# Half of the value transposes moved behind the diagonal products, two groups of the projection later

## The reference

```
def hgrn_branch(h, w_in, lb, g_onorm, w_out, s0):
    proj = h @ w_in                                  # (T, 4096): q, f, value, z
    q, fpre, inp, z = jnp.split(proj, 4, axis=-1)
    ...                                              # gates, 8 heads of 128 columns
    o, S = hgrn2_chunked(q, k, v, log_f, s0)         # o_t = q_t S_t, S_t = diag(f_t) S_{t-1} + k_t^T v_t
    o = rms_norm(o, g_onorm).reshape(b, T, BRANCH)
    return (o * jax.nn.silu(z)) @ w_out, S
```

## Time and profile before

| | |
|---|---|
| median of three executions | 1053.92 us |
| the profiled execution | 1053.46 us |
| its span on the core | 1051.7 us, so 1.76 us lie around it |
| TensorE busy | 1036.7 us, 99% |
| VectorE busy | 718.3 us, 68% |
| ScalarE busy | 378.4 us, 36% |
| chain that ended last | 91% TensorE, 5% VectorE |

### The profile page before, as it was taken

One profiled execution on the slowest core, in us unless ns is written; L12 is line 12 of the kernel. 1 busy time (PEld: TensorE's weight loads), 2 busy tenths in 40 slices (PEclk: granted clock), 3 DMA queues, 4 the chain that ended last, 5 costly groups with the idle time before them and its releaser, 6 DMA issues.

```text
span 1051.7 us, 20604 instructions
## 1 busy us (share of the span) xinstructions
PE 1036.7 (99%) x8085; PEld 980.8 (93%) x8085; DVE 718.3 (68%) x1289; ACT 378.4 (36%) x720; POOL 37.7 (4%) x53
## 2 busy tenths in 40 slices
PE   6999999999999999999999999999999999999998
PEld 6999999999999978899999999999999999997886
DVE  7799677677676826662759577585967759587355
ACT  7443433333333624442224241332424133272222
POOL 1000000000000000000101001010100101010000
PEclk9999999999999999999999999999999999999999
DMA  7102121112112243221221212121121212143064
GB/s 232 38 21 81 41 72 49 40 53 67 40 40 80 106 153 121 101 80 41 61 61 44 61 43 60 42 60 52 50 60 42 60 42 60 50 137 128 12 244 172
DMA packets 95430, 78.78 MB, mean 75 GB/s; under 512 B 2967, under 2 KB 86744, under 8 KB 95386
## 3 DMA queue, kind: packets, MB, share of 16 engines
q1 hardware_dynamic: 77498, 69.19, 20.6%
q10 hardware_dynamic: 17888, 8.98, 2.9%
HBM read 64.72 MB, written 13.44 MB: 74 GB/s over the span
## 4 chain that ended last, share of the span: by engine, by line
PE 91%; DVE 5%; DMA 2%; issue 1%; ACT 1%; SPq 0%; DVEq 0%
PE bank L656 35%; PE bank L704 24%; PE bank L796 13%; PE bank L1010 4%; PE bank L676 2%; PE bank L886 2%; DMA wraw<-in_w_in 1%; PE bank L959 1%; PE bank L966 1%; PE bank L968 1%; PE bank L880 1%; PE bank L916 1%; PE bank L778 1%; PE bank L894 1%; PE bank L954 1%
## 5 line engine op out<-in xcount | busy, mean ns | idle before, releaser
L656 PE MATMUL bank<-reg_a,wsplit 128*128 128x352 f32 x2304 | 387.7, 325 | 0.6 <-ACT arena L1377 0.6
L656 PEld LDWEIGHTS bank<-reg_a,wsplit 128*128 128x128 f32 x2304 | 368.5, 188 | 2.8 <-issue 0.9
L704 PE MATMUL bank<-reg_a,wsplit 128*128 128x264 f32 x1344 | 165.4, 284 | 0.0
L704 PEld LDWEIGHTS bank<-reg_a,wsplit 128*128 128x128 f32 x1344 | 164.1, 188 | 0.0
L704 PE MATMUL bank<-reg_b,w_ring 128*128 128x264 f32 x1008 | 124.7, 284 | 0.6 <-DVE wraw L1703 0.6
L704 PEld LDWEIGHTS bank<-reg_b,w_ring 128*128 128x128 f32 x1008 | 123.3, 188 | 0.8 <-DVE wraw L1703 0.8
L796 PE MATMUL bank<-reg_b,reg_a 128*128 128x512 f32 x288 | 69.3, 396 | 0.0
L796 PEld LDWEIGHTS bank<-reg_b,reg_a 128*128 128x128 f32 x288 | 53.7, 188 | 12.7 <-issue 0.4
L1769 DVE TENSOR_TENSOR arena<-arena,bank 128x264 f32<-128x264 f32 x84 | 34.8, 427 | 33.5 <-PE bank L704 32.4
L1211 ACT ACTIVATE w_ring<-wraw 128x512 fp32r<-128x512 f32 x42 | 26.1, 631 | 68.7 <-PE bank L704 68.7
L1233 ACT ACTIVATE arena<-bank 128x264 f32<-128x264 f32 x84 | 32.0, 389 | 49.9 <-PE bank L704 45.2
(11 more groups left out here) (279 smaller groups left out, 1514.6 us busy)
## 6 DMA issues: line engine op xcount, KB each, us to landing
wraw<-in_w_in SPq DMA_DIRECT2D x64, 512.0 KB, 4.1
arena<-in_x_prompt SPq DMA_DIRECT2D x16, 512.0 KB, 4.0
wraw<-in_w_out SPq DMA_DIRECT2D x8, 512.0 KB, 3.3
w_out_raw<-in_w_out SPq DMA_DIRECT2D x8, 512.0 KB, 5.1
arena<-in_w_out SPq DMA_DIRECT2D x8, 512.0 KB, 4.6
x_scratch<-arena SPq DMA_DIRECT2D x8, 512.0 KB, 2.6
arena<-in_state_hgrn ACTq DMA_DIRECT2D x8, 512.0 KB, 3.8
out<-arena ACTq DMA_DIRECT2D x8, 512.0 KB, 2.9
```

Source lines behind the costliest of these rows:

```text
L656: mm = nc.tensor.matmul(bank[b][:, 0:CH], w[wi][:, k, :], rhs[hi], start=(k == 0 and i == 0), stop=(k == KT - 1 and i == 2))
L704: mm = nc.tensor.matmul(bank[banks[q]][:, 0:QT], w[wi][:, k, :], B_OP[name][hi][:, k, q * QT:(q + 1) * QT], start=(start and k == 0 and i ...
```

## The change

In `rec` of TensorE the 8 value transposes of stage 1 are cut in two halves. The first four (bank 5) and the stacked sample values stay. The other four (bank 6) are issued in stage 3, behind the diagonal products, and raise a new event `values_turned`. ScalarE copies the first half in stage 1 as before; the second half it copies in its stage 3, behind the evacuation of group 3, after a wait for `values_turned`; that copy now raises ScalarE's event "vt". In head 7 (`final`) everything stays in stage 1, with the new wait ahead of the second copy. No instruction is added or dropped on the data path.

```diff
+            def turn_values(half):
+
+                for c in range(CK // 2):
+                    mm = nc.tensor.transpose(bank[5 + half][:, tokens(c)], r_vr[:, tokens(half * CK // 2 + c)], ident[:, :])
+                if half:
+                    mm.then_inc(values_turned, 1)
+
-            def rec(h, s, last):
+            def rec(h, s, last, final=False):
...
                     pe.wait_ge(VR.sem, VR.at(h, "v3"))
-                    for c in range(CK):
-                        nc.tensor.transpose(bank[5 + c // 4][:, tokens(c % 4)], r_vr[:, tokens(c)], ident[:, :])
+                    turn_values(0)
+                    if final:
+                        turn_values(1)
                     nc.tensor.transpose(bank[7][0:STK, 128:256], r_vt[:, CK * P:CK * P + STK], ident[:, :]).then_inc(PR.now("vt"), 1)
...
                     nc.tensor.matmul(bank[7][0:NSAMP, 0:NSAMP], r_K[:, NP:], r_Q[:, NP:], start=True,
                                      stop=True).then_inc(PR.now("dg"), 1)
+                    if not final:
+                        turn_values(1)
...
+            def values(h):
+
+                act.wait_ge(values_turned, h + 1)
+                A(r_vt[:, 512:NP], bank[6][:, :], ACT.Copy).then_inc(AR.now("vt"), 1)
+
...
-                    for half in range(2):
-                        ins = A(r_vt[:, half * 512:(half + 1) * 512], bank[5 + half][:, :], ACT.Copy)
-                    ins.then_inc(AR.now("vt"), 1)
+                    A(r_vt[:, 0:512], bank[5][:, :], ACT.Copy)
+                    if final:
+                        values(h)
                     if last is not None:
                         turn_hi(last)
+                elif s == 3:
+                    values(h)
```

More of the change, by code:

```diff
@@ L322, in build @@
         E_ACT = Events(sem("last_head_act"), ["fa", "k", "qc"])
+        values_turned = sem("values_turned")
         ot_done, o_rdy, o_hi, o_lo = sem("ot_done"), sem("o_rdy"), sem("o_hi"), sem("o_lo")
@@ L1047, in _ @@
                 runs[s]()
-                rec(H, s, KT - 2)
+                rec(H, s, KT - 2, True)
             runs[2]()
@@ L1051, in _ @@
             low(0)
-            rec(H, 3, KT - 2)
+            rec(H, 3, KT - 2, True)
             for k in (1, 2):
```

## The result

The change makes the kernel slower by a little: median 1055.73 us over 19 runs against 1053.92 us over 19 runs of the kernel before, ratio 1.0017 with a 95% interval of 1.0010 to 1.0023. That is +1.8 us. The profiled execution of after took 1055.11 us with a span of 1053.4 us, 1.65 us more than before.

The account below looks back on a forecast made before the run. TensorE, busy for all of each 61.6 us turn, was taken to bound the kernel, so only its pauses count. 1053.46 us profiled plus 1.87 gave 1055.33, median 1055.8 us (+0.18%), range 1053.8 to 1057.1.

Parts of the forecast that it names:

- The lead: Stage 1, heads 0 to 6: without four transposes TensorE starts group 2, and would start group 3, 0.435 us earlier.
- The pause: Ahead of group 3, heads 1 to 6: TensorE waits for split_lo, 0.505 us minus margin each, 1.87 us in sum.
- the margin: Time from split_lo's end to group 3's first load in before: 0.16 to 0.21 us in heads 1 to 6.
- The release: Time from split_lo's end to the start of group 3's starved load: taken as 0.12 us, lower end 0.06.
- given back by the restart: Group 3's first load to second matmul: 0.26 us when starved against 0.32 in a running stream, 0.05 in favour.
- "vs": TensorE's second wait, ahead of the diagonal products (line 916): margin 0.95 us, no cost unless the lead passed about 0.8.
- Stage 3: Four transposes behind the diagonal products add 0.435 us; difference at the width switch taken as 0, bounds -1.4 to +1.4.
- rival 3: Border behind the diagonal products: the transposes fill the width switch, 1.4 us come back, 1054.4 us; chance 0.13.
- ScalarE: Second copy moved to stage 3: cost 0, with 2.7 us of cover; head 7's extra wait 0 to 0.12 us, taken as 0.
- rival 1: Stage 0 on VectorE: split_lo moves along to an earlier time, so no pause, 1053.9 us; chance 0.15.
- rival 2: Border between transposes and group 4: width switch paid twice, 0.2 us in seven heads more, 1057.2 us; chance 0.20.
- rival 4: Faster by over 0.2%, through a pause that exists now and goes; none found in the loop; chance 0.04.

Follow-up runs that it names:

- all_moved: All eight value transposes and both copies in stage 3, against the kernel before: median 1057.89 us, ratio 1.0035, turn 62.316 us.
- all_early: All eight value transposes and both copies in stage 3, with split_lo earlier on VectorE, against the kernel before: median 1053.43 us, ratio 0.9995.
- act_only: Kernel before with only ScalarE's copy of the second half of the values moved to stage 3, all transposes in stage 1: 1054.19 us, ratio 1.0001.
- moved_early: The change plus split_lo earlier on VectorE in heads 0 to 6, timed against the kernel before: 1053.85 us, ratio 0.9996.
- one_moved: One of the eight value transposes in stage 3 instead of four, against the kernel before: 1054.09 us, ratio 0.9999.
- before_filler: Kernel before with a useless VectorE copy of 666 columns at the start of stage 0 in heads 0 to 6: 1055.63 us, ratio 1.0012.

## Why the prediction was right

**What bounds it** held: nothing but a pause of TensorE moved the time. The kernel lost 1.65 us in the profiled execution, and head 0 and the six turns behind it account for all of it (-0.04 us and +1.70; what lies before and behind them is the same within 0.03).

**The lead** of 0.435 us: four transposes fewer in stage 1 took 0.44 us less. The Trainium skill (TensorE: Matmul & The Clock Gate, Back-to-back issue gap) would have made the lead an estimated 0.32 us and the loss 1.2 us; the transposes kept their 109 ns and the loss came out above that.

**The pause** was put at 0.505 minus the margin, 0.31 us in the mean and 1.87 in sum. Between stage 1 and stage 3 the six heads took 0.28 to 0.36 us longer than before, 1.96 in sum. The release of 0.12 us, chosen over 0.06, was right for the loop: 0.12 in every head with a pause. The reason given for the choice, the same line with the same pair of waits in front, does not carry, though: head 0 of all_moved has both, too, and its release was 0.05. So there was some luck in this term. The 0.05 given back by the restart came out as 0.268 against 0.317 from load to second matmul. What made it 1.96 instead of 1.87 are hundredths in each head: 0.01 us was lost ahead of the diagonal products in the heads with a pause (3.782 us from the second matmul of group 3 to their first load, instead of 3.772), and the release was 0.124 and not 0.12. `split_lo` ended up to 0.05 us earlier or later than before in single heads, but in the sum of the six this is nothing. The idle time was forecast at 0.35 us, released by VectorE; the profile shows 0.28 to 0.36 and calls it "issue".

**"vs"** cost nothing, as forecast. Line 2131 (before 2113) ended at 571.58 and the load of the diagonal products started at 572.42, 0.84 us later, where 0.95 - 0.13 = 0.82 was reckoned. The point from which it would matter was put too low, at a lead of about 0.8 us: in all_early the lead was 0.87 and the wait still cost nothing. How much further it would go no run shows.

**Stage 3** is the term that was mis-sized, in the harmless direction: taken as 0 besides the 0.435, it was 0.04 us less in each of seven heads, 0.3 us in sum, a fifth of what rival 3 had offered. 1.96 - 0.3 is the 1.65 measured. For the profiled execution the forecast was 1055.33 us, and it took 1055.11. That the forecast for the median, 1055.8 us, came within 0.1 us of the 1055.73 measured is partly luck: the profiled execution lay 0.62 us under the median this time, where 0.46 had been taken.

**ScalarE** was free, by act_only and by its rows in head 1. The copy starts at 574.38 (574.7 was reckoned in the times of before, where TensorE ended the diagonal products 0.2 us later) and is done 3.3 us before the next evacuation:

```profile
574.38 0.60 ACT L1441 ACTIVATE arena<-bank 128x512 f32<-128x512 f32 x1 [1.38 <-PE bank L901]
578.24 0.47 ACT L1386 ACTIVATE arena<-bank 128x352 f32<-128x352 f32 x1 [3.26 <-PE bank L657]
```

The new wait in head 7 showed nothing: from there to the end the span is the same to 0.02 us.

**The rivals.** `split_lo` did not move along (rival 1): its mean distance from stage 0 is the same to 0.001 us. The switch was not paid twice (rival 2), and the transposes filled a fifth of it (rival 3). No gain was found (rival 4).

**A better version?** moved_early and all_early have the shortest turns, 0.04 and 0.05 us under before, and ratios of 0.9996 and 0.9995. Their traces put the gain at 0.3 us; the timed runs cannot tell it from nothing.

## What to carry to other kernels

On an engine that is always busy, moving work behind a wait is only free if what answers the wait has more to spare than the work that is moved and the restart together (here 0.07 us: 0.12 of release less 0.05 given back). one_moved shows that the restart counts: 0.109 us of work moved against a margin of 0.19 in before and about 0.14 in that run still made small pauses. Look for the first wait between the old and the new place and subtract, for each pass of the loop. The margin is to be read from the starts of single instructions, since a busy share of 99% and an engine that idles over a quarter of the time both hide it. And where a pause is found, first ask whether the answering engine has the work in a needlessly late place: here its order, not its load, made the loss.

## What was not expected of the hardware

- The release of a starved weight load took two values from the same source line: 0.05 us in head 0, which is unrolled (507.21 - 507.16 in all_moved), and 0.12 us in the hardware loop (569.52 - 569.40). The loop does not explain it by itself: a load of this line behind ScalarE took 0.12 us in unrolled code as well. What makes the difference is not shown.
- Going from 32 columns wide to full width costs 0.04 us less if a transpose of 128 columns comes first than if a projection matmul of 352 does (stage 3 grew by 0.39 us for 0.435 us of transposes, and with eight of them by 0.83 for 0.87: once per border).
- A pause at a wait can carry the name "issue" in the profile (the change, before_filler), and a pause that is there anyway can carry the name of an engine (all_early). Only the length compared with another kernel tells.
